# The order of the query tiles in the two attentions of the second mixer, turned round

## What is computed

```
# differential attention, 4 heads, two maps m of width 64 each, block of 128 queries
logits = q_m k_m^T * 64**-0.5 + bias[bucket(k - q)]       # for m = 0, 1
logits = where(key // 64 <= query // 64, logits, -1e30)
attn   = softmax(logits_0) - lam * softmax(logits_1)
o      = attn @ v                                         # v of width 128
# then an rms norm over the 128 columns of each head

# latent attention, 8 heads of width 96 (64 + 32 with rotary positions)
logits = q k^T * 96**-0.5, masked in the same way
o      = softmax(logits) @ v                              # v of width 64
```

## Time and profile before

| | us |
|---|---|
| median of 3 runs | 3249.36 |
| profiled execution | 3252.2 |
| its span | 3250.9 |
| TensorE busy | 3010.0 (93%) |
| VectorE busy | 1578.3 (49%) |
| ScalarE busy | 1016.5 (31%) |
| granted TensorE clock, mean | 0.952 |

### The profile page before, as it was taken

The page is one execution under the profiler, slowest core; times in us unless marked ns, Lnnn a source line. Parts: engine busy times, 40 slices in busy tenths (PEclk is TensorE's granted clock), DMA queues, the critical chain, the costliest instruction groups (busy, mean ns, idle before and its releaser), DMA issues.

```text
span 3250.9 us, 35127 instructions
## 1 busy us (share of the span) xinstructions
PE 3010.0 (93%) x14780; PEld 2509.8 (77%) x14780; DVE 1578.3 (49%) x1984; ACT 1016.5 (31%) x1378; POOL 136.5 (4%) x73
## 2 busy tenths in 40 slices
PE   8999969997999999999999777789999999999988
PEld 6878857885888888887878667678878888888777
DVE  4256756625444434436442574565434544454444
ACT  3243344523111111114231465566321112111241
POOL 0012221013000000001000000000000000000000
PEclk9999988998999999999999888788999999999999
DMA  4111120020211111111221000000211111111111
GB/s 157 51 39 53 53 98 1 20 92 13 71 46 46 52 52 46 46 52 40 60 89 52 14 7 22 1 1 1 104 39 51 47 53 46 46 47 57 46 46 65
DMA packets 43213, 156.16 MB, mean 48 GB/s; under 512 B 5136, under 2 KB 5648, under 8 KB 43056
## 3 DMA queue, kind: packets, MB, share of 16 engines
q1 hardware_dynamic: 43056, 153.90, 14.6%
HBM read 136.85 MB, written 17.04 MB: 47 GB/s over the span
## 4 chain that ended last, share of the span: by engine, by line
PE 85%; DVE 7%; ACT 4%; issue 2%; DMA 1%; POOL 0%; SPq 0%; DVEq 0%; ACTq 0%
PE PS L272 22%; PE PS L274 21%; PE PS L276 21%; PE PS L472 2%; PE PS L471 2%; PE PS L470 2%; PE PS L1165 2%; PE PS L686 2%; PE PS L2439 1%; PE PS L1135 1%; PE PS L2064 1%; PE PS L1150 1%; PE PS L2034 1%; PE PS L2430 1%; DVE Y L426 0%
## 5 line engine op out<-in xcount | busy, mean ns | idle before, releaser
L272 PE MATMUL PS<-u_hi_f,w_hi 128*128 128x512 f32 x1408 | 438.7, 393 | 25.8 <-DVE u_lo_f L387 12.8
L274 PE MATMUL PS<-u_lo_f,w_hi 128*128 128x512 f32 x1408 | 436.7, 391 | 0.0
L276 PE MATMUL PS<-u_hi_f,w_lo 128*128 128x512 f32 x1408 | 436.2, 391 | 0.0
L266 DVE TENSOR_TENSOR w_lo<-w_raw,w_hi 128x1024 fp32r<-128x1024 f32 x215 | 273.9, 1282 | 316.5 <-ACT w_hi L260 316.4
L260 ACT ACTIVATE w_hi<-w_raw 128x1024 fp32r<-128x1024 f32 x215 | 225.9, 1052 | 612.8 <-PE PS L276 476.0
L272 PEld LDWEIGHTS PS<-u_hi_f,w_hi 128*128 128x128 f32 x1408 | 265.7, 189 | 85.7 <-DVE w_lo L266 12.5
L274 PEld LDWEIGHTS PS<-u_lo_f,w_hi 128*128 128x128 f32 x1408 | 266.4, 189 | 56.0
L276 PEld LDWEIGHTS PS<-u_hi_f,w_lo 128*128 128x128 f32 x1408 | 266.3, 189 | 55.8
L272 PE MATMUL PS<-f_ah,w_hi 128*128 128x512 f32 x704 | 219.5, 393 | 10.2 <-DVE f_al L1576 10.2
L274 PE MATMUL PS<-f_al,w_hi 128*128 128x512 f32 x704 | 218.5, 392 | 0.0
L276 PE MATMUL PS<-f_ah,w_lo 128*128 128x512 f32 x704 | 218.5, 392 | 0.0
(11 more groups left out here) (380 smaller groups left out, 5026.7 us busy)
## 6 DMA issues: line engine op xcount, KB each, us to landing
w_raw<-in_weights SPq DMA_DIRECT2D x215, 512.0 KB, 3.6
H<-in_x_t SPq DMA_DIRECT2D x16, 512.0 KB, 4.2
stick_kept<-stick_stage SPq DMA_DIRECT2D x12, 512.0 KB, 2.9
mixer<-stick_kept SPq DMA_DIRECT2D x9, 512.0 KB, 9.1
h_kept<-H SPq DMA_DIRECT2D x8, 512.0 KB, 5.9
H<-h_kept SPq DMA_DIRECT2D x8, 512.0 KB, 7.7
out_t<-H SPq DMA_DIRECT2D x8, 512.0 KB, 3.0
bias_lines<-df_line SPq DMA_DIRECT2D x16, 143.9 KB, 8.4
```

What stands on the lines that cost most here:

```text
L266: dve.tensor_tensor(self.w_lo[i][:], self.w_raw[i][:], self.w_hi[i][:].bitcast(F32), ALU.subtract).then_inc(*self.s("w_lo").up(g))
L272: ins = e.matmul(banks[i], lh, rh[i], start=first, stop=False)
L274: ins = e.matmul(banks[i], lh, rl[i], start=False, stop=False)
L276: ins = e.matmul(banks[i], ll, rh[i], start=False, stop=last)
```

## The change

Both item functions give the tiles in the other direction: even heads from tile 7 down, odd heads up. As item 0 of the differential attention is now tile 7, which reads all keys, it waits for both halves of the key parts.

```
     def diff_item(self, n):
         h, t = n // TT, n % TT
-        return h, t if h % 2 == 0 else TT - 1 - t
+        return h, TT - 1 - t if h % 2 == 0 else t
...
                 qh, ql, kh, kl = self.df_sets[h % 2]
-                if n == 0:
-                    pe.wait_ge(*self.s("head_lo").at("diff", 0, 1, 0))
-                elif n == 1:
-                    pe.wait_ge(*self.s("head_lo").at("diff", 0, 1, 1))
-                elif n % TT == 0:
+                if n % TT == 0:
                     pe.wait_ge(*self.s("head_lo").at("diff", h, 1, 1))
...
     def mla_item(self, n):
         h, t = n // TT, n % TT
-        return h, t if h % 2 == 0 else TT - 1 - t
+        return h, TT - 1 - t if h % 2 == 0 else t
```

## The result

| us | before | after |
|---|---|---|
| median (20 runs each) | 3243.7 (3238.3 to 3253.9) | 3259.5 (3254.9 to 3267.4) |
| ratio, 95% interval | 1 | 1.0047 (1.0039 to 1.0056) |
| profiled execution / its span | 3252.2 / 3250.9 | 3259.8 / 3258.5 |
| granted clock, mean | 0.952 | 0.947 |

What follows compares the result with a forecast made beforehand. TensorE was 85% of the chain, but a serial ScalarE and VectorE chain held the first steps of heads preparing the next. Differential +10.9 and latent +3.7 gave +14.6 on the median 3249.4: 3264.0 us, range 3250 to 3277.

Steps and rivals of the forecast that it cites:

- (a): Differential attention up to its first bias: starting on tile 7 needs the last key half and a longer score; +2.1 us.
- (b): Latent attention up to its first maximum: the tile 7 score has six passes against three short ones; +1.8 us.
- (c): Differential heads that prepare the next: two up and one down become two down and one up; +7.8 us.
- (g): Clock in both attentions: half rate at first heads' large tiles and last heads' small tiles; +7.5 us, bounds 0 to +16.
- (d): Latent heads that prepare the next: four up and three down become four down and three up; +1.6 us.
- (e): Differential last head and tail: the head goes up without a preparation and ends on tile 7; -3.5 us.
- (f): Latent last head and tail: the head goes up and the tail consumes tiles 4 to 7; -2.7 us.
- The rival in which the first D loses its TensorE work: First down-going heads are TensorE-bound, so shorter by 8.9 us (differential) and 6.8 (latent); 3240.8 us, chance 0.10.
- a last U over 29, then a step of small tiles has a floor that I don't see: Sign of a wrong forecast: the differential last head, going up, taking over 29 us where 24.2 was forecast at full clock.
- first bias before 1823: Sign of a wrong forecast: the differential attention's first bias before 1823 us, where about 1823.9 was expected.
- The mark that TensorE would idle more in the first steps of each attention: Sign of a right forecast: TensorE's idle time in each attention's first three steps above that before; no size given.

Runs made afterwards that it cites:

- e6: Changed kernel plus unread extra matmuls in the first three differential steps and around the first latent preparation and steps, to keep TensorE awake; 3257.7 us, 1.0033 of before.
- e7: Kernel before with every head of both attentions going down from tile 7; 3274.3 us, 1.0093 of before.
- e9: Changed kernel plus one unread extra matmul ahead of each wait for a copied chunk in the differential attention (sums over chunks not kept); 3256.5 us, 1.0039 of before.
- e4: Kernel before with only the last head of each attention turned to go up, ending on tile 7; 3240.1 us, 0.9992 of before.
- e8: Kernel before with all heads up but each attention's last down, and differential head 0's output norm three steps later; 3231.9 us, 0.9956 of before.

## Why the prediction was right in sign, and where it was off

The forecast was +14.6; the medians say +15.8, the windows +16.75. (The time that it gave, 3264.0, is 4.5 too high, as the median of 20 runs before is 5.7 below that of the first three.) Term by term:

| step | forecast | measured, windows | 
|---|---|---|
| (a) fill, differential | +2.1 | +1.0 |
| (b) fill, latent | +1.8 | +2.0, with all that lies between |
| (c) prepared heads, diff, with 3 of (g) | +10.8 | +9.8 |
| (d) prepared heads, latent, with 2 of (g) | +3.6 | +4.7 |
| (e) last head and tail, diff, with 1.5 of (g) | -2.0 | +2.7 |
| (f) last head and tail, latent, with 1 of (g) | -1.7 | -3.5 |

That the sum came so near is in part luck: misses of +4.7 in (e), +1.1 in (d) and +0.2 in (b) stand against -1.1, -1.0 and -1.8 in (a), (c) and (f).

**(c) held in size, and the reason given is shown for the first head.** Two D and a U with a preparation cost 9.8 more than two U and a D. The first three steps of the new first D have the length of the chain whether TensorE is at 0.60 or 1.00 (17.85 and 17.84, e6), and behind another head they are 18.10 where it ended on small tiles (e7) and 19.32 where it ended on large ones (before), 1.2 apart and not the 8.9 of the rival. The rival in which the first D loses its TensorE work is out by both. Two of its parts cancelled in part: the third head was 51.36 and not 47 to 49, and the U between them was 35.93 and not 37 to 39. The third head has two causes. Its first three steps take 23.81, since the output norm lies on the chain there, and behind it, in the third step, TensorE's turns and products of the t = 7 of the head ahead, which start after a wait of 3.25 us, in a step with a granted clock of 0.62. So this D isn't the chain of ScalarE and VectorE alone: in e7, behind a head that ended on small tiles, the same three steps take 20.60. And the clock falls again in its last two steps, which are 2.9 us longer than those of e6 (5.86 and 5.59 for 4.86 and 3.69). The latent first three steps repeat closely in these two orders: 14.43 to 14.45 in every D and 11.15 to 11.16 in every U, but for head 0 (14.24 and 10.97).

**(e) is the term that missed most: not its work, but the clock in it.** The forecast put the last U at 24.2 and its tail at 14.7, together 38.9 at full clock. The head at full clock is 22.50 (e9), and the tail is 15.8 to 16.1 at 0.90 and 0.89 (here, e4), which is 38.3 to 38.6. The 1.5 us that (g) put on this head is the mis-sized term: it is 6.8 (29.31 against 22.50). I had taken it as a spell of half rate over the first small tiles. Windows of the changed kernel, cut where the pitch of the matmuls changes, and the first matmuls of a score on either side:

```profile
1945.64:1968.76 23.12, 20.28 (x89) 14.50 (x88) 15.52 (x49) 13.34 (x33) 0.00 (x0) 0.53 0.00 1
1968.76:1974.95 6.19, 5.50 (x43) 4.24 (x43) 5.05 (x12) 3.67 (x7) 0.00 (x0) 1.00 0.00 0
```

```profile
1963.75 0.79 PE L2030 MATMUL PS<-df_kh,df_qh 64*128 64x512 f32 x2
...
1968.76 0.50 PE L2030 MATMUL PS<-df_kh,df_qh 64*128 64x512 f32 x2
```

TensorE stayed at 1.2 GHz, but for moments, for 23 of the head's 29 us, although it shows 20.28 us busy of 23.12: at half rate the same matmuls fill nearly twice the time (the passes of a score over 512 keys start 0.43 us apart, for 0.23 behind the cut). In e4 the same head runs at 1.00 throughout behind a U that ended on t = 7, and in e9 behind the same D with the added matmuls. So the clock that it starts with decides much: 0.50 here, at the end of a D whose last step ran at 0.50, and 1.00 in e4 and e9. The small end of the D doesn't settle it alone, as e6 starts at 1.00 behind the same D; it then falls to 0.53 in the fourth step and takes 27.72. What makes the clock fall in one profile and not in the other isn't shown. The mark "a last U over 29, then a step of small tiles has a floor that I don't see" was reached; there is no floor, since the steps of e9 are as short as forecast (2.5 to 4.3 us), and the cause is the clock.

By the Trainium skill, "TensorE: Matmul & The Clock Gate", "HAM oscillation — how this bites in real kernels", a matmul kernel whose bursts of matmuls are shorter than the DMA waits between them starts every burst at the lower clock. This trace agrees in the outcome only: t = 0 to 5 run for 23 us at 0.53, but the waits between their matmuls, for copies by ScalarE, are 0.58 us at the longest.

**(g) as a whole.** Forecast 7.5. Shown by experiment is 6.8 in the last U, 2.4 in the fourth step of the first head (7.77 to 5.34) and 2.9 in the last two steps of the third (e6). The forecast had no term for that last one. In the tail it is about 1: the last wait for a copy, 1.96 in the earlier trace rows, is still there, and the 16 matmuls of the products behind it run at 0.197 us each, between the two pitches (at 0.129 they would take 2.1):

```profile
1986.69 0.66 PE L2043 MATMUL PS<-ident,H 128*128 128x128 f32 x4 [1.95 <-ACT df_at L2083]
...
1987.18 3.15 PE L2060 MATMUL PS<-mixer,df_at 128*128 128x128 f32 x16
```

In the latent attention heads of the same code differ by up to 1.6 us between profiles (31.39 here, 29.81 in e9 for the third head), and the granted clock of single steps shows where. The first three steps of each D below take 14.43, and TensorE is busy all through its fourth and fifth:

| latent D | head, us | fourth step: us, clock | fifth step: us, clock |
|---|---|---|---|
| second head, before | 28.18 | 3.32, 0.53 | 3.86, 1.00 |
| fourth head, before | 29.81 | 4.17, 0.50 | 4.64, 0.88 |
| third head, changed kernel | 31.39 | 3.47, 0.50 | 6.23, 0.52 |
| second head, e7 | 30.71 | 4.42, 0.50 | 4.71, 0.87 |

The clock falls in the fourth step of a D, and how soon it is back decides whether the head takes 28 or 31 us. So of what the forecast called the price of a latent D, 1.6 in (d), 1.1 is gone in the one head where the clock is back at once (28.18, against 29.3 on the mean).

**(a)** came at half its price, and the mark "first bias before 1823" fell: 1813.48, or 1822.87 if the earlier start of the stage is put back. The score of t = 7 ran at full clock (1.00 in the first window) and not at the half rate that my figure had room for. **(f)** was better than forecast, 12.96 and 9.27 with TensorE busy in all of it: 22.2 against 23.0. **(d)** was right in size, within what the profiles scatter. The mark that TensorE would idle more in the first steps of each attention held in the differential one (9.7 us idle against 7.0) and fell in the latent one (1.7 against 3.9): the latent stretch runs at 0.50 before and after, and at that clock the larger tiles' matmuls fill the time.

What stays open: why the clock falls and returns when it does. An e7 latent D behind a D is 30.7 us and not the 28.2 of the second head before for 2.0 us in its fourth and fifth steps, where the clock is low, and 0.6 in its last (1.71 for 1.13), which no run takes apart.

## What to carry to other kernels

Where a serial side chain (here the next head's norms) is woven into a loop over tiles of growing size, lay it beside the small tiles, and lay the large ones where nothing else is on the chain; e8 does so and takes 0.9956 of the time before, where the changed kernel takes 1.0047. The clock of an engine that idles is paid by the tiles that come after (6.8 us in the last U, 2.4 behind the sparse start), so price a new order by what stands behind each sparse stretch, and expect that the lower clock can last through nearly all the small tiles. Compare profiles from a mark inside the program: here the stretch ahead of the change moves by 10 us between executions, more than half of the effect.

## What the runs showed of the hardware

- TensorE at a granted clock of 0.53 for 23.1 us while its rows show it busy 88% of that time (1945.64 to 1968.76): a busy engine in the profile is no sign of a full clock, and the busy time of such a stretch is not its work.
- Filler is not free even where TensorE waits: one matmul of 256 columns before each copy's wait cost the first head 5.1 us (50.01 against 44.87), which is more than the 2.4 that the half clock cost it by e6, and the clock wasn't back in time either (0.64 in the fourth step).
- Two latent heads of one kind, both D with a preparation and first three steps of 14.43 us, take 28.18 and 31.39 us; the granted clock of their fifth step is 1.00 and 0.52. A profile of one execution shows one such case only.
